# Weighing attention values in three float32r passes of split operands instead of one plain float32 product

## The reference

```python
_, sel = lax.top_k(score, n_sel)
valid = sel <= q_pos[None, :, None]
...
logits = jnp.einsum('bthd,btkd->bhtk', qb, kg).astype(jnp.float32) * attn_scale
bias = rel_bias_table[_t5_bucket(q_pos[None, :, None] - sel)]
logits = logits + jnp.moveaxis(bias, -1, 1).astype(jnp.float32)
logits = jnp.where(valid[:, None], logits, -jnp.inf)
p = jax.nn.softmax(logits, axis=-1).astype(vg.dtype)
return jnp.einsum('bhtk,btkd->bthd', p, vg)
```

## Time and profile before

| | us |
|---|---|
| median of 3 runs | 3522.06 |
| lowest and highest | 3521.34, 3523.16 |
| span of the profiled execution | 3521.0 |
| PE busy in it | 3273.7 (93%) |
| VectorE busy | 1516.9 (43%) |
| ScalarE busy | 888.9 (25%) |
| POOL busy | 1277.4 (36%) |

### The profile page before, as it was taken

The page is one execution under the profiler, slowest core; times in us unless marked ns, Lnnn a source line. Parts: engine busy times, 40 slices in busy tenths (PEclk is TensorE's granted clock), DMA queues, the critical chain, the costliest instruction groups (busy, mean ns, idle before and its releaser), DMA issues.

```text
span 3521.0 us, 34997 instructions
## 1 busy us (share of the span) xinstructions
PE 3273.7 (93%) x13583; PEld 2480.0 (70%) x13594; DVE 1516.9 (43%) x2274; ACT 888.9 (25%) x1239; POOL 1277.4 (36%) x603
## 2 busy tenths in 40 slices
PE   7999989999777999999996998899998899999999
PEld 5787775587555788888884766565446688878787
DVE  2799946472734312122127102457872322222222
ACT  3322126402334100100104333545454200000000
POOL 2254333244512333433431332743311334444443
PEclk9899999999898999999998999999899999999999
DMA  2123310042100111111111123521111011111111
GB/s 98 31 90 111 111 42 1 28 160 105 54 24 24 42 48 48 48 48 48 48 48 32 54 72 106 155 73 56 42 57 42 30 48 48 42 48 48 48 48 72
DMA packets 66839, 209.14 MB, mean 59 GB/s; under 512 B 7084, under 2 KB 18516, under 8 KB 65976
## 3 DMA queue, kind: packets, MB, share of 16 engines
q1 hardware_dynamic: 39552, 141.31, 13.0%
q10 hardware_dynamic: 27192, 66.54, 5.2%
HBM read 171.11 MB, written 36.46 MB: 59 GB/s over the span
## 4 chain that ended last, share of the span: by engine, by line
PE 84%; DVE 9%; ACT 5%; issue 1%; POOL 1%; ACTq 0%; DMA 0%; POOLq 0%; DVEq 0%
PE ps L514 24%; PE ps L516 23%; PE ps L515 23%; PE ps L552 3%; PE ps L715 2%; PE ps L1020 2%; PE ps L1008 1%; DVE x L1632 1%; PE ps L994 1%; DVE y L1631 1%; PE ps L993 1%; PE ps L705 1%; PE ps L982 1%; DVE rows L1964 1%; DVE hidden_lo L1847 1%
## 5 line engine op out<-in xcount | busy, mean ns | idle before, releaser
L403 POOL TENSOR_TENSOR w_hi<-w_raw,zero 128x1024 fp32r<-128x1024 f32 x210 | 405.8, 1932 | 1750.9 <-PE ps L516 1744.1
L514 PE MATMUL ps<-normed_hi,w_hi 128*128 128x512 f32 x1488 | 589.6, 396 | 43.1 <-DVE normed_lo L1616 29.4
L515 PE MATMUL ps<-normed_lo,w_hi 128*128 128x512 f32 x1488 | 584.3, 393 | 0.0
L516 PE MATMUL ps<-normed_hi,w_lo 128*128 128x512 f32 x1488 | 584.1, 393 | 0.0
L406 POOL TENSOR_TENSOR w_lo<-w_raw,w_hi 128x1024 fp32r<-128x1024 f32 x210 | 557.8, 2656 | 16.5
L514 PE MATMUL ps<-hidden_hi,w_hi 128*128 128x512 f32 x864 | 342.5, 396 | 30.4 <-DVE hidden_lo L2040 18.8
L514 PEld LDWEIGHTS ps<-normed_hi,w_hi 128*128 128x128 f32 x1488 | 282.8, 190 | 108.4 <-issue 34.8
L516 PE MATMUL ps<-hidden_hi,w_lo 128*128 128x512 f32 x864 | 340.3, 394 | 0.0
L515 PE MATMUL ps<-hidden_lo,w_hi 128*128 128x512 f32 x864 | 340.2, 394 | 0.0
L515 PEld LDWEIGHTS ps<-normed_lo,w_hi 128*128 128x128 f32 x1488 | 282.9, 190 | 61.1 <-issue 2.2
L516 PEld LDWEIGHTS ps<-normed_hi,w_lo 128*128 128x128 f32 x1488 | 282.5, 190 | 60.0
(11 more groups left out here) (360 smaller groups left out, 5426.5 us busy)
## 6 DMA issues: line engine op xcount, KB each, us to landing
w_raw<-weights_dram SPq DMA_DIRECT2D x228, 512.0 KB, 3.5
gates_scratch<-tmp ACTq DMA_DIRECT2D x24, 512.0 KB, 2.7
gated<-gates_scratch ACTq DMA_DIRECT2D x24, 512.0 KB, 5.6
head_raw<-diff_qk_scratch SPq DMA_DIRECT2D x32, 256.0 KB, 4.0
x_in<-x_dram ACTq DMA_DIRECT2D x4, 1024.0 KB, 10.9
x<-x_dram ACTq DMA_DIRECT2D x1, 4096.0 KB, 14.4
diff_qk_scratch<-d_out ACTq DMA_DIRECT2D x8, 512.0 KB, 2.7
mla_nope_scratch<-g_nope ACTq DMA_DIRECT2D x8, 512.0 KB, 2.9
```

The source lines that it names most:

```text
L403: nc.gpsimd.tensor_tensor(w_hi[s][:], raw[s][:], zero[:, 0:1].broadcast_to([P, 1024]), ALU.add).then_inc(w_rounded, 1)
L514: nc.tensor.matmul(out, sh, mh, start=start, stop=False)
L515: nc.tensor.matmul(out, sh, ml, start=False, stop=False)
L516: return nc.tensor.matmul(out, sl, mh, start=False, stop=stop)
```

## The change

`value` and `probs_t` become pairs of a float32r high part and a low part. ScalarE's copies now write the high parts. VectorE makes the low parts: one of 128x1024 for value, between key's low part and the top-k, and 72 of 128x512 for the probabilities, in a new function `rest_of_probs`. It subtracts the high part in SBUF from the transposed probabilities in PSUM. The product becomes three passes through `product`. PE's waits for ScalarE's copies (`pt_out`, `value_out`) become waits for VectorE's low parts (`probs_rest`, `value_rest`).

```diff
-        value = at("value", BR + 32 * KB, [P, NT, P])
+        value = pair("value", BR + 32 * KB, [P, NT, P])
...
-        probs_t = [at(f"probs_t{i}", BR + 40 * KB + 2 * KB * i, [P, HALF]) for i in range(2)]
+        probs_t = [pair(f"probs_t{i}", BR + 40 * KB + 4 * KB * i, [P, HALF]) for i in range(2)]
...
                 if n_tr >= 2:
-                    pe.wait_ge(pt_out, n_tr - 1)
+                    pe.wait_ge(probs_rest, n_tr - 1)
...
-                pe.wait_ge(pt_out, n_tr + 1)
-
-                nc.tensor.matmul(ps[:, 6 + group % 2, :], value[:, j, :], probs_t[n_tr % 2][:], start=j == 0,
-                                 stop=j == group // 2).then_inc(pv_done, 1)
+                pe.wait_ge(probs_rest, n_tr + 1)
+
+                product(ps[:, 6 + group % 2, :], tuple(v[:, j, :] for v in value), tuple(v[:] for v in probs_t[n_tr % 2]),
+                        j == 0, j == group // 2).then_inc(pv_done, 1)
...
-            nc.scalar.activation(value[:], wide(2).rearrange("p (j n) -> p j n", j=NT), ACT.Copy).then_inc(value_out, 1)
+            nc.scalar.activation(value[0][:], wide(2).rearrange("p (j n) -> p j n", j=NT), ACT.Copy).then_inc(value_out, 1)
...
-                        nc.scalar.activation(probs_t[n_tr % 2][:], ps[:, 4 + n_tr % 2, :], ACT.Copy).then_inc(pt_out, 1)
+                        nc.scalar.activation(probs_t[n_tr % 2][0][:], ps[:, 4 + n_tr % 2, :], ACT.Copy).then_inc(pt_out, 1)
...
             in_lo(3, [part[:] for part in key], wide(0))
+            dve.wait_ge(value_out, 1)
+            tt(value[1][:], wide(2).rearrange("p (j n) -> p j n", j=NT), value[0][:].bitcast(F32),
+               ALU.subtract).then_inc(value_rest, 1)
...
+            def rest_of_probs(group, n):
+                for j in tiles_of(group, n):
+                    n_tr = tiles_before(group) + j
+                    dve.wait_ge(pt_out, n_tr + 1)
+                    tt(probs_t[n_tr % 2][1][:], ps[:, 4 + n_tr % 2, :], probs_t[n_tr % 2][0][:].bitcast(F32),
+                       ALU.subtract).then_inc(probs_rest, 1)
+
...
                     if n == 0 and group:
                         mix_out_lo(group - 1)
+                    rest_of_probs(group, n)
                     if more and n:
                         mix_inverse(unit - 1)
```

More of the change, by code:

```diff
@@ L305, in program @@
         shifted_in, flipped, bias_done = sem("shifted_in"), sem("flipped"), sem("bias_done")
-        value_out = sem("value_out")
+        value_out, value_rest, probs_rest = sem("value_out"), sem("value_rest"), sem("probs_rest")
         masks_ready = sem("masks_ready")
@@ L633, in _ @@
             pe.wait_ge(pooled_ready, POOL_GROUPS)
-            pe.wait_ge(value_out, 1)
+            pe.wait_ge(value_rest, 1)
             for i, g in enumerate(POOL_ORDER):
```

## The result

The changed kernel takes **3549.5 us** (median of four runs, 3548.3 to 3553.5), the kernel before 3522.6 in the same comparison: a ratio of 1.0078, 95% interval 1.0064 to 1.0093: slower, clear of noise, and by less than 2%. The forecast was 3548, with a range of 3534 to 3560. The profiled execution has a span of 3548.1 us, 27.1 more than before.

The account below looks back on a forecast made before the run. PE was taken as the bound in groups 6 to 14, by a small distance, and as already waiting in groups 0 to 5. Losses of 6.6, 17.8 and 1.75 us sum to 26: 3521 + 26 + 1.1 = 3548 us, range 3534 to 3560.

Parts of the forecast that it names:

- The price of a product: Product at L715: 0.86 us plain, 0.69 as three passes; 0.17 saved, times 72: 12.2 us if nothing else moves.
- (a) Low part of value: Before the top-k: pushes it back 1.2 us, covered by VectorE's later 39.35 us idle time, so priced at nothing.
- (b) T to V: Between transposes (T) and value product (V): V starts at T + 2.05 us, before 1.28, if VectorE is free.
- (c) The order: On VectorE: the inverse that POOL's scaling needs queues behind the low parts' wait; before, it ran a full PE step earlier.
- (d) The port: VectorE operations reading two SBUF operands, or scaling in SBUF, wait for POOL to finish: some 8 or 9 of 26 us.
- The walk: Group 8 laid out step by step, losing 2.25 us; likewise groups 6 to 14 lose 17.8 together, the last group 1.75.
- Groups 0 to 5: Short rows at the stage's start: one low part of 0.68 us enters the softmax chain per tile; together 6.6 us lost.
- The clock rival: TensorE's clock falls more often: two to five stretches, each about 1.3 us; +6, 3554 us; chance 0.15.
- PE's busy share: Sign in the trace after: PE busy 65 to 80% in groups 5 to 9.
- the 3570 rival: Split passes run no closer than 0.39 us, their records' length, adding 22 us: 3570 us; chance 0.02.
- The hidden and the partly hidden ones: Hidden: low parts hide, 12 us come off, 3510, chance 0.06. Partly: boundary costs eat savings, 3517 to 3529, chance 0.07.
- that without the port: The waits bite, but VectorE and POOL slip past each other without port delays: 3539 us; chance 0.15.

Follow-up runs that it names:

- e1: Changed kernel with the high parts in all three passes and no low parts of the probabilities made: 3516.9 us against 3519.5 for the kernel before.
- e7: Inverse-first kernel (e4) with the pass that reads the low part of the probabilities run last and alone waiting for VectorE: 3524.8 us.
- e4: Changed kernel with VectorE computing the inverse of the unit before ahead of the low parts, not behind them: 3533.3 us.
- e5: Changed kernel with only the query's low part moved from n = 1 to n = 2, behind the low part of the probabilities: 3547.0 us.
- e8: Against the kernel before: groups 0 to 7 stay plain; groups 8 to 15 three passes, low part's last, inverse first, query's low part at n = 2: 3515.5 us, ratio 0.9981.
- e2: Changed kernel with the plain float32 product waiting only for ScalarE's copy; low parts of the probabilities still made but not read: 3536.5 us.
- e10: As e2 (plain product, low parts made and not read), but with the inverse ahead of the low parts: 3524.8 us.

## Why the prediction was right, step by step

Four kernels in a row split the loss of the stage: passes -5.8 us (e1); low parts, in a good place and read last, +6.2 (e7 less e1); the product waiting for the low part with its first pass, +11.2 (e4 less e7); the inverse behind the low part, port included, +15.9 (changed less e4). Sum 27.4. The forecast sum was 26. Each term is the difference of two traces and holds clock stretches of up to 1.4 us each; the 11.2 hold some 3 us of them, less one stretch in e7's group 6.

The mechanism came as forecast. That the total came within 1.5 us is in part luck: the short groups lost 2.4 us more than forecast, the long ones 1.0 and the last 0.2 less, and the clock's two effects on the short groups (below) cancel in part.

- **The price of a product.** 0.86 to 0.69 us was right for a step that nothing holds up: the last group of e1 saved 1.32 us over eight products, 0.165 each. 72 x 0.17 = 12.2 "if nothing else moves" was too large even then; the passes alone gave 5.8 us in the stage. PE waits for rows in the short groups (8.3 us in e1's stage, 6.3 before), so a quicker product there only lengthens the wait, and groups 9 to 14 gave 0.07 to 0.14 a product. The sum didn't suffer, because it went by the walk through the groups.
- **(a) Low part of value.** Right: 1.22 us ahead of the top-k, and VectorE's idle time before the stage went from 39.35 to 38.24 us.
- **(b) T to V.** Right at 2.01 us; 11.2 us of the loss by e4 and e7.
- **(c) The order.** Right, and the largest: 15.9 us.
- **(d) The port.** Right in kind; its share at the query's low part was put at 0.3 to 0.8 us in each of eight groups, 2.4 to 6.4 together. The trace has 0.52 to 1.05 in each of groups 6 to 13, 6.1 together, and e5 gave 7.4 us in groups 6 to 14, of which up to 1.9 may be the new place itself. At the boundary the scaling ended 0.28 to 0.55 us behind POOL (forecast 0.35 to 0.55). What was missed is that the port is not a term of its own. It is met so often only because the inverse comes late, and e4 freed both. One reading was wrong though its conclusion holds: key_lo was not in the middle of POOL's instruction, it ended 0.32 us behind it (135.34 + 1.23 against 134.35 + 1.90), so that row alone can't tell a wait from none. e4 can: 40 of its 72 low parts run beside POOL and none takes over 693 ns.
- **The walk.** Forecast and measured for groups 6 to 14, us over before: 3.35/3.19, 2.9/2.76, 2.25/2.16, 2.4/2.32, 2.0/1.91, 1.85/1.79, 1.25/1.15, 1.3/1.02, 0.5/0.50; together 17.8/16.8. Last group 1.75/1.57.
- **Groups 0 to 5, the step that was off.** 6.6 forecast, 9.0 measured; by group 0.6/0.79, 0.8/1.80, 1.0/3.12, 1.3/1.24, 1.0/0.24, 1.9/1.85. The excess is in groups 1 and 2, and most of it is the clock. Before, PE was at 1.2 GHz from about 507 to 517 us and again in group 4; after, from about 503 to 534 and not in group 4. With filler, at 2.4 GHz from 512 us on, groups 0 to 3 lost 3.6 us, and the forecast had 3.7; without it 7.0. Group 4's small loss is the clock too, the other way: 10.64 us against 10.40 with a fall in it, but against 9.02 without one (e8) it is 1.6. So the clock added 3.4 us in groups 0 to 3 and hid 1.4 in group 4, which the walk had not in it. The clock rival had counted more falls; there was one, longer.
- **Other stages to the tenth of a microsecond.** Wrong. The stage began 1.8 us earlier and the rest took 1.5 us longer, within what executions of unchanged code differ by.
- **PE's busy share.** Put at 65 to 80% in groups 5 to 9. It was 70, 75, 80, 85 and 83%: a little high in groups 8 and 9.
- **The rivals.** The passes ran 0.23 us apart, so the 3570 rival is out. Its price was also added wrongly: 72 x (3 x 0.39 - 0.86) = 22 us is over the plain product, but the forecast to which it was added already had passes of 0.69 us. Over that it is 72 x 0.48 = 35, and the rival would be 3583. The hidden and the partly hidden ones are out by e2, which loses 19 us without any product that waits; that without the port by the longer L1708 and L1739.

## What to carry to other kernels

Before a step is put into an engine's program, look at what is queued behind the wait that it brings: here 49 us of new work cost 5 us of the stage in one place and 19 in another, one statement apart (e10, e2). A value that releases other engines goes ahead of work that waits. When a sum of passes needs a late operand, run the passes that don't need it first, and wait with the last one alone. And use a quicker operation only in the stretch where its engine is the bound: the short groups kept the old product in the one version with a full result that gained. e7, with three passes in all groups, was level with the kernel before (1.0006, 0.9995 to 1.0017).

## What the runs showed of the hardware

The meeting of VectorE and GpSimd reaches down to tiny operations. In group 8, L1729, a tensor_tensor on 128x1 from SBUF, took 0.51 us beside POOL's instruction (603.53 + 1.25 = 604.78; it ended at 604.81) and 0.16 alone, and the negated maximum behind it (L1730) waited for it. It met POOL before the change too, up to 0.54 us (L1726). The new low parts have one operand in PSUM. In the changed kernel none of the 72 runs beside POOL; in e4 40 do and take 668 to 693 ns, the other 32 677 to 692. The Trainium skill (SBUF — State Buffer, "SBUF: two separate sides") describes an exclusive lock for VectorE operations with two SBUF inputs; by that rule, the trace agrees.

The stretch that TensorE spends at 1.2 GHz at the stage's start depends on what it does there. In the changed kernel it was busy for 0.23 us of 501 to 504 and the clock fell at 503; in the kernel before it was busy for 0.08 us of 538 to 540 and the clock fell at 541. The same four groups ran at 0.66 of full clock in the changed kernel and at about 0.96 with filler in the waits, 33.8 against 30.4 us. Single falls cost 0.9 us in group 1 (e1), where PE waits anyhow, at least 1.1 in group 6 (e1), where it is the bound, and 1.4 in group 4. The Trainium skill (TensorE: Matmul & The Clock Gate, "HAM oscillation") lists idling between groups of matmuls as the cause of such falls; by that rule, the two falls above agree. That filler in one place was followed by falls in two others is shown by one trace alone, and why it was is open.
